# Feed-forward stages of a float32 network: the high weights multiply both parts of the rows in one 512-column product

## What is computed

```python
def rmsnorm(x, g):
    y = x * lax.rsqrt(jnp.mean(x * x, axis=-1, keepdims=True) + EPS)
    return y * g

def swiglu_2(xn, wg, wu, wd):            # wg, wu: 1024 x 2816, wd: 2816 x 1024
    return (jax.nn.silu(xn @ wg) * (xn @ wu)) @ wd

x = x + y                                # y: what the layer's mixer gives
x = x + swiglu_2(rmsnorm(x, norm_ffn[i]), ff_w_gate[i], ff_w_up[i], ff_w_down[i])
```

## Time and profile before

| | |
|---|---|
| median of 3 runs | 2932.46 us (2931.55 to 2935.47) |
| span of the profiled execution | 2930.2 us |
| around the span, against the median | 2.3 us |
| TensorE busy, matmuls | 2883.4 us (98%), 20144 |
| VectorE, ScalarE, GpSimd busy | 2031.7, 1626.6, 300.7 us |
| chain that ended last | TensorE 96% |
| moved by DMA | 613.26 MB, mean 209 GB/s |
| one 1 MB panel, issue to landing (L245) | 4.7 to 5.3 us |

### The profile page before, as it was taken

The page is one execution under the profiler, slowest core; times in us unless marked ns, Lnnn a source line. Parts: engine busy times, 40 slices in busy tenths (PEclk is TensorE's granted clock), DMA queues, the critical chain, the costliest instruction groups (busy, mean ns, idle before and its releaser), DMA issues.

```text
span 2930.2 us, 46621 instructions
## 1 busy us (share of the span) xinstructions
PE 2883.4 (98%) x20144; PEld 2666.9 (91%) x20144; DVE 2031.7 (69%) x1842; ACT 1626.6 (56%) x1603; POOL 300.7 (10%) x224
## 2 busy tenths in 40 slices
PE   8999999999999999999999999999999999999999
PEld 8999999999988888888888696999899999896999
DVE  6787665678768888888888775654665565575653
ACT  6456544545657767767767562544754454362542
POOL 1130210113010000000000002210011011002110
PEclk9999999999999999999999999999999999999999
DMA  7444555544449989889989640556365646540553
GB/s 237 159 140 155 183 180 180 187 145 144 159 173 370 350 343 375 348 339 353 377 333 373 204 154 15 180 177 210 111 187 176 198 145 186 189 144 30 158 184 119
DMA packets 359731, 613.26 MB, mean 209 GB/s; under 512 B 11520, under 2 KB 323926, under 8 KB 324577
## 3 DMA queue, kind: packets, MB, share of 16 engines
q1 hardware_dynamic: 355936, 597.99, 58.5%
q10 hardware_dynamic: 3104, 12.10, 1.2%
q0 software_dynamic: 480, 0.12, 0.0%
HBM read 608.99 MB, written 1.05 MB: 208 GB/s over the span
## 4 chain that ended last, share of the span: by engine, by line
PE 96%; DVE 1%; ACT 1%; DMA 0%; issue 0%; POOL 0%; ACTq 0%; SPq 0%; DVEq 0%; POOLq 0%
PE ps L329 19%; PE ps L331 19%; PE ps L330 19%; PE ps L1272 5%; PE ps L1274 5%; PE ps L1273 5%; PE ps L1248 3%; PE ps L1250 3%; PE ps L1249 3%; PE ps L1813 2%; PE ps L689 2%; PE ps L1828 2%; PE ps L1322 1%; PE ps L1781 1%; PE ps L1769 1%; PE ps L1291 1%
## 5 line engine op out<-in xcount | busy, mean ns | idle before, releaser
L273 DVE TENSOR_TENSOR wlo<-raw,whi 128x2048 fp32r<-128x2048 f32 (+2 forms) x574 | 1317.0, 2300 | 451.8 <-ACT whi L262 432.6
L262 ACT ACTIVATE whi<-raw 128x2048 fp32r<-128x2048 f32 (+2 forms) x574 | 1084.4, 1891 | 259.9 <-PE ps L331 136.3
L329 PE MATMUL ps<-HX,whi 128*128 128x256 f32 x1808 | 521.4, 288 | 16.3 <-DVE wlo L273 11.6
L331 PE MATMUL ps<-HX,wlo 128*128 128x256 f32 x1808 | 512.5, 283 | 0.0
L330 PE MATMUL ps<-HX,whi 128*128 128x256 f32 x1808 | 512.4, 283 | 0.0
L329 PE MATMUL ps<-HXB,whi 128*128 128x256 f32 x1760 | 501.3, 285 | 2.7 <-DVE HXB L448 2.7
L330 PE MATMUL ps<-HXB,whi 128*128 128x256 f32 x1760 | 498.6, 283 | 0.0
L331 PE MATMUL ps<-HXB,wlo 128*128 128x256 f32 x1760 | 498.6, 283 | 0.0
L329 PEld LDWEIGHTS ps<-HX,whi 128*128 128x128 f32 x1808 | 347.8, 192 | 22.6 <-ACT HX L524 10.3
L330 PEld LDWEIGHTS ps<-HX,whi 128*128 128x128 f32 x1808 | 347.9, 192 | 3.4 <-issue 3.3
L331 PEld LDWEIGHTS ps<-HX,wlo 128*128 128x128 f32 x1808 | 347.7, 192 | 0.0
(11 more groups left out here) (337 smaller groups left out, 4228.8 us busy)
## 6 DMA issues: line engine op xcount, KB each, us to landing
raw<-in_c_experts SPq DMA_DIRECT2D x264, 1024.0 KB, 4.9
raw<-in_w_in SPq DMA_DIRECT2D x71, 1024.0 KB, 5.0
raw<-in_ff_w_gate SPq DMA_DIRECT2D x44, 1024.0 KB, 5.3
raw<-in_ff_w_up SPq DMA_DIRECT2D x44, 1024.0 KB, 5.3
raw<-in_ff_w_down SPq DMA_DIRECT2D x32, 1024.0 KB, 5.2
raw<-in_dense_w SPq DMA_DIRECT2D x30, 1024.0 KB, 5.3
raw<-in_hy_w_in SPq DMA_DIRECT2D x24, 1024.0 KB, 5.3
raw<-in_ff_w_down SPq DMA_DIRECT2D x16, 768.0 KB, 4.7
```

The costliest lines, as they stand in the source:

```text
L262: e.activation(m.whi[:, i % NSPLIT, 0:n], m.raw[:, i % NRAW, 0:n], ACT.Copy).then_inc(*k.up("act", "hi", i))
L273: e.tensor_tensor(m.wlo[:, i % NRAW, 0:n], m.raw[:, i % NRAW, 0:n], hi, ALU.subtract).then_inc(*k.up("dve", "lo", i))
L329: e.matmul(o, wh, xh, start=first and t == k0, stop=False)
L331: i = e.matmul(o, wl, xh, start=False, stop=final and t == k1 - 1)
```

## The change

In the five stages wh·xh and wh·xl become one matmul: the two parts of a chunk, x[:, :, t, :], stream as 512 columns past the same wh block and fill a whole bank: columns 0 to 255 get wh·xh, 256 to 511 get wh·xl. wl·xh is a 256-column matmul as before and adds into the first half. The two halves of the bank have to be added by somebody afterwards. A block a or b now needs two banks, which `Book.pair` hands out (an even one and its neighbour); y's need one as before, and use all of it.

```diff
+def pe_both_rows(e, k, o, w, c, x, k0, k1, kx, first=True, final=True, fresh=None):
+    for t in range(k0, k1):
+        wh, wl = (v[:, t, c:c + 128] for v in w)
+        if fresh:
+            e.wait_ge(*k.at(*fresh, kx + t))
+        e.matmul(o[:, :], wh, x[:, :, kx + t, :], start=first and t == k0, stop=False)
+        i = e.matmul(o[:, 0:L], wl, x[:, 0, kx + t, :], start=False, stop=final and t == k1 - 1)
+def pe_wide_gemm(e, k, m, s, name, x, j, fresh=None):
+    i = pe_panel(e, k, m)
+    w = weights(m, i, 8, 256)
+    o = pe_take_pair(e, k, m, "g", s, name, j)
+    pe_both_rows(e, k, o[0], w, 0, x, 0, 8, 0, fresh=fresh)
+    pe_both_rows(e, k, o[1], w, 128, x, 0, 8, 0).then_inc(*k.up("mm", "g", s, name, j))
 def pe_ffn(e, k, m, s, last, after=None):
-        pe_gemm(e, k, m, s, "a", m.HXB, [j], fresh=None if j else ("hx", last))
+        pe_wide_gemm(e, k, m, s, "a", m.HXB, j, fresh=None if j else ("hx", last))
...
-                mm = pe_weights_still(e, k, o[c][:, 0:L], w, 128 * c, m.HID, ...)
+                mm = pe_both_rows(e, k, o[c], w, 128 * c, m.HID, ...)
+def act_low_sums(e, k, m, s, name, j):
+    e.wait_ge(*k.at("g", s, name, j))
...
+    e.activation(low_sums(m, name, j), pair_halves(k, m, "g", s, name, j)[1], ACT.Copy)...
 def pool_ffn(e, k, m, s, last):
+        e.wait_ge(*k.at("sum", s, "a", j))
+        e.wait_ge(*k.at("rstd", last))
+        e.tensor_tensor(v, v, m.wide_rs, ALU.mult).then_inc(*k.up("pool", "a normed", s, j))
         e.wait_ge(*k.at("sil", s, j))
         e.tensor_tensor(v, v, m.wide_rs, ALU.mult).then_inc(*k.up("pool", "sil normed", s, j))
 def dve_ffn(e, k, m, panels, s, last, nxt, after=None):
-        dve_times_norm(e, k, m, s, last, "a", j, sil)
+        if j:
+            dve_hidden_low(e, k, m, s, j - 1)
+        e.wait_ge(*k.at("low", s, "a", j))
+        e.tensor_tensor(sil..., low_sums(m, "a", j), pair_halves(k, m, "g", s, "a", j)[0], ALU.add)...
         dve_panel(e, k, m, panels)
+        e.wait_ge(*k.at("low", s, "b", j))
+        e.tensor_tensor(b, b, pair_halves(k, m, "g", s, "b", j)[0], ALU.add)...
         e.wait_ge(*k.at("sil normed", s, j))
-        e.tensor_tensor(hf, sil, ps(k, m, "g", s, "b", j)[:, :], ALU.mult)...
+        e.tensor_tensor(hf..., sil..., b, ALU.mult)...
...
             e.wait_ge(*k.at("y", s, c))
-            e.tensor_tensor(m.X[:, c, :], m.X[:, c, :], ps(k, m, "y", s, c)[:, 0:L], ALU.add)...
+            e.tensor_tensor(m.X[:, c, :], m.X[:, c, :], o[:, 0:L], ALU.add).then_inc(*k.up("dve"))
+            e.wait_ge(*k.own("dve"))
+            e.tensor_tensor(m.X[:, c, :], m.X[:, c, :], o[:, L:2 * L], ALU.add)...
```

More of the change, by code:

```diff
@@ L102, in bank, with pair @@
         self.turn += 1
-        self.before[group], self.owner[b] = self.owner[b], group
+        self.before[group], self.owner[b] = [self.owner[b]], group
+        self.bank_of[group] = b
+        return b
+    def pair(self, *group):
+        while self.turn % 2 or self.turn % 8 in self.held or self.turn % 8 + 1 in self.held:
+            self.turn += 1
+        b = self.turn % 8
+        self.turn += 2
+        self.before[group] = self.owner[b:b + 2]
+        self.owner[b:b + 2] = [group, group]
         self.bank_of[group] = b
@@ L304, in pe_take, with pe_take_pair, pair_halves @@
     b = k.bank(*group)
-    if k.before[group]:
-        e.wait_ge(*k.at("free", *k.before[group]))
+    for owner in k.before[group]:
+        if owner:
+            e.wait_ge(*k.at("free", *owner))
     return m.psum[b]
+def pe_take_pair(e, k, m, *group):
+    b = k.pair(*group)
+    for owner in dict.fromkeys(k.before[group]):
+        if owner:
+            e.wait_ge(*k.at("free", *owner))
+    return m.psum[b], m.psum[b + 1]
+def pair_halves(k, m, *group):
+    b = k.bank_of.get(group, 0)
+    both = m.banks[:, 512 * b:512 * b + 1024].rearrange("p (c h n) -> p c h n", c=2, h=2)
+    return both[:, :, 0, :], both[:, :, 1, :]
 def pe_hold(e, k, m, *group):
@@ L1041, in act_ffn @@
             act_rstd(e, k, m, last, m.rs[:, :])
[L1042 to L1049 removed]
+        else:
+            act_hidden_high(e, k, m, s, j - 1)
+            if after:
+                after(j - 1)
+        act_low_sums(e, k, m, s, "a", j)
+        act_panel(e, k, m, panels)
+        e.wait_ge(*k.at("a normed", s, j))
+        e.activation(sil, sil, ACT.Silu).then_inc(*k.up("act", "sil", s, j))
+        act_low_sums(e, k, m, s, "b", j)
+    act_hidden_high(e, k, m, s, 10)
+    if after:
+        after(10)
     for j in range(4):
@@ L2599, in pool_program @@
     pool_sums(e, k, m, "hgrn0")
-    pool_ffn(e, k, m, "ffn0")
+    pool_ffn(e, k, m, "ffn0", "hgrn0")
     pool_sums(e, k, m, "ffn0")
```

69 lines of the change are left out of this document (42 added, 27 removed).

## The result

The changed kernel takes 2903.47 us (median of 4 runs, 2898.49 to 2904.63); beside it the kernel before took 2932.81 us. The ratio is 0.9896, with a 95% interval of 0.9884 to 0.9907: 1.0% faster, 29.3 us. The median lies inside the 8-of-10 range of 2895.5 to 2907, but outside the forecast's own range of 2896 to 2901, which had 77%, and short of the 2905 to 2912 of the third rival. The profiled execution took 2904.63 us, its span 2902.8, against 2930.2 before: 27.4 us less, where the sum of the prediction had 33.65.

A forecast was written before the change was run, and what follows sets the result against it. TensorE's matmul start distances were taken to bound the kernel; 34.3 - 0.2 - 0.45 = 33.65 us saved takes 2932.46 to 2898.8 us. Own range 2896 to 2901 (77%), 8 of 10 within 2895.5 to 2907.

The forecast's parts named there:

- the third rival: Wide matmul 5 ns dearer beside the narrow one, or GpSimd's slow case costs 6 us: 2905 to 2912 us; 8%.
- What bounds the kernel: TensorE, busy in 98% of the span; time is the sum of distances between matmul starts.
- 227 + 120 = 347 ns: Five feed-forward stages: a wide plus a narrow matmul replace three of 120 ns, 360 ns a triple.
- fourth rival: Most of the 13 ns belongs to something kept, such as weight changes: time between 2932.9 and 2898.8 us; 2%.
- 13 ns per triple: Saving for each of 2640 triples in the feed-forward stages, 34.3 us in all.
- The first blocks: First block of ffn3 saves 0.14 us less (input wait, lower clock); whole loss over five stages rounded to 0.2 us.
- The readers: Other engines' added work per turn costs nothing: their chain goes round in 8.0 us where TensorE takes 11.1.
- The down projection's second addition: Costs nothing at ends of ffn0 to ffn3, covered by 0.4 us; adds 0.45 us at the kernel's end.
- The readers stop TensorE: Rival: TensorE waits 1.29 us every turn for a pair's copy and sum, 71 us, giving 2970 us; 5%.
- Two runs cost nothing: Answers a rival: reading two runs costs about a matmul's start, pair 360 ns, time stays 2932.5 plus 0.5; 5%.
- The fifth: Rival: a wide matmul hides more of the weight change than the experts' do, 2885 to 2895 us; 3%.
- upper bound of 430 ns: Wide matmul priced as a plain float32 one of 512 columns, which would cost 502 us.

The follow-up runs named there:

- the layout with one run: Changed kernel with HXB and HID laid out by chunk, then part, so the wide matmul reads one run of 512 columns: 2901.0 us, ratio 0.9892.
- The turned order: Changed kernel with the order turned around in every other pair (wide, narrow, narrow, wide): 2902.72 us, ratio 0.9895.
- the kernel with two more: Changed kernel with both of GpSimd's multiplications of a turn done twice: 2971.6 us, ratio 1.0129.
- a break each turn: Changed kernel with one more plain float32 matmul of 128 columns, into its own bank, ending each of 55 turns: 2925.49 us, ratio 0.9975.

## Why the prediction was right, point by point

The mechanism and the size of most terms held. How near the median of 2903.47 came to 2898.8 is partly luck of the draw: by the change's own profile it would be some 2897 us with every pair short, and some 2911 with all of ffn1 to ffn4 long.

**What bounds the kernel.** Right. TensorE is still busy in 98% with 2.7 us of idle time in the five stages, and putting the third matmul back gives 1.0001 of the time before.

**227 + 120 = 347 ns.** The mechanism is right and the size nearly so. The pair takes 346.67 ns in the good case, and the read of two runs costs nothing (the layout with one run has the same two values). What was saved is what a matmul costs beyond its columns, as the prediction said. Whether this belongs to the start or to the weight load that goes with each matmul stays open: the change takes away 2640 of both, and the prediction's fourth rival reckoned with loads that stay. The sign that the prediction gave, starts 227 and 120 ns apart in turn, came as 230 and 117. The mis-sized term is "13 ns per triple": 13.33 in short stretches and 6.67 in long ones, in this profile 10.4 on average. The third rival, a wide matmul some 5 ns dearer beside a narrow one, had 8%, and it came true in part: 6.67 ns, but only in 1120 of the 2560 pairs and, outside ffn0, not always the same ones. The prediction took its two prices from a row of only narrow and a row of only wide matmuls, and the sum of the two did not have to be the price of the alternation. The turned order, 348.33, lies between.

**The first blocks.** They saved 0.35 us in four stages where 16 x 13 ns each, 0.8, was expected (of the 0.2 held back, 0.14 was ffn3's). In ffn3 I expected 0.1, and 1.45 us went, mostly because the slow piece of the earlier trace rows was missing. The kernel after at that place (start of ffn3, after the wait for the last chunk):

```profile
2337.50 0.50 PE L370 MATMUL ps<-HXB,whi 128*128 128x512 f32 x1 [1.45 <-DVE HXB L498]
...
2338.35 0.44 PE L370 MATMUL ps<-HXB,whi 128*128 128x512 f32 x1
...
2339.14 0.40 PE L370 MATMUL ps<-HXB,whi 128*128 128x512 f32 x1
...
2339.49 0.40 PE L370 MATMUL ps<-HXB,whi 128*128 128x512 f32 x1
```

The wait is the same 1.45 us, but the four pairs behind it take only 1.64 us together; then it is 0.35 a pair. Before, the matmuls after the wait went 213 ns apart, 256 columns at 1.2 GHz, half the full clock. I had taken the clock of one profile for a property of the place.

**The readers.** Right, and tested from both sides. The turn is TensorE's, each sum waits for a copy and each copy for a product. The prediction took 0.05 us for a handover; its rows give 0.03 (523.32 + 0.42 = 523.74 to 523.77), which makes its 8.0 us some 7.8 and changes nothing. It left it open whether GpSimd falls beside a panel once or twice: once, in its second operation. In the timeline of VectorE and GpSimd, answering to the earlier trace rows:

```profile
2388.37 1.30 POOL L1136 TENSOR_TENSOR work<-work,rs 128x512 f32<-128x512 f32 x1 [6.49 <-DVE work L1157]
...
2389.41 2.41 DVE L284 TENSOR_TENSOR wlo<-raw,whi 128x2048 fp32r<-128x2048 f32 x1 [1.12 <-ACT whi L273]
...
2390.41 2.56 POOL L1138 TENSOR_TENSOR work<-work,rs 128x512 f32<-128x512 f32 x1 [0.74 <-ACT work L1118]
```

1.30 us nearly alone, 2.56 beside the panel, and in the kernel with two more 3.27, there the first operation and right behind a panel's start. By the Trainium skill, "SBUF — State Buffer", section "SBUF: two separate sides", the two engines lock a shared port pair against each other; the trace agrees, since the lengthened operation ends about when the panel plus its own 1.3 us do (2389.41 + 2.41 + 1.3 = 2393.1 against 2392.97). The panel pays too, 2.41 against 2.29, but not for this operation: the first one still ran when the panel started (2388.37 + 1.30 = 2389.67). In the kernel with two more, where the first operation starts 0.16 us behind the panel, the panel takes 2.29.

**The down projection's second addition.** Right at both places. At the end of ffn0 in the kernel after, VectorE, ScalarE, VectorE, answering to the earlier trace rows:

```profile
517.42 0.42 DVE L1177 TENSOR_TENSOR X<-X,ps 128x256 f32<-128x256 f32 x1 [0.81 <-PE ps L371]
517.88 0.42 DVE L1179 TENSOR_TENSOR X<-X,ps 128x256 f32<-128x256 f32 x1
...
518.33 0.51 ACT L489 ACTIVATE HX<-X,par 128x256 fp32r<-128x256 f32 x1 [1.26 <-DVE X L1179]
...
518.88 0.48 DVE L498 SCALAR_TENSOR_TENSOR HX<-X,par,HX 128x256 fp32r<-128x256 f32 x1 [0.18 <-ACT HX L489]
```

The last chunk is ready at 519.36; TensorE began at 517.22 and needs it at 519.74. 0.4 us of cover is what was foretold. And at the end of the kernel, where it is in full view, answering to the earlier trace rows:

```profile
2899.55 0.42 DVE L1177 TENSOR_TENSOR X<-X,ps 128x256 f32<-128x256 f32 x1 [1.24 <-PE ps L371]
2900.01 0.42 DVE L1179 TENSOR_TENSOR X<-X,ps 128x256 f32<-128x256 f32 x1
```

0.46 us between the two additions, for 0.45.

**The rivals.** The readers stop TensorE in every stage only with two more GpSimd operations (2971.6; that the rival's sum was 2970 is chance, its 1.29 us a turn had another cause). Two runs cost nothing. That most of the 13 ns would stay is refuted by the short pairs. The Trainium skill has a fixed cost of about 2.5 ns per matmul at full clock ("TensorE: Matmul & The Clock Gate", section "Wait — 56ns, not 53.3ns?"). The trace disagrees for matmuls like these: the third matmul, with its load and with the same columns still streamed, was worth 13.3 ns. The fifth, more saved than 13.3 ns, shows in no stretch.

**A bound that was misread.** The prediction's upper bound of 430 ns for a plain float32 matmul of 512 columns is half of what it should be. The trace lists such a matmul as two rows: the x8 of the earlier trace rows are the four matmuls of `pe_filters`, (2547.41 - 2543.97)/4 = 860 ns each. Nothing else in the sum used it.

**What stays open.** What sets short or long in strict alternation. The value holds until something else passes through TensorE, goes when two neighbours are alike, and comes in a period of four with a break each turn. In ffn0 its pieces came the same in every such profile without breaks, in the later stages they did not. An alignment of the two lengths to something that runs by its own clock would fit, and so might the banks, but neither was tried. Open is also what of the 13.3 ns is the weight load's. Whether the lower clock between ffn2 and ffn3 belongs to executions or to kernels is open too; the mean clocks leave little room for it in the gain.

## What to carry to other kernels

Where TensorE is never idle, price a change of matmuls by the distance from start to start, and take the price of a mixed sequence from a mixed sequence: the sum of two pure ones was right at best and 6.67 ns per pair too low at worst. Merging two matmuls that share their weights into a wider one saves what a matmul and its weight load cost beyond the columns, here 13 ns of 120, and the work that it moves to other engines is free as long as their round trip (9.6 us) stays under TensorE's turn (11.1). Testing that with one operation more and two more shows how far away the edge is, and a stage with other work in its turns (ffn0 here) meets it first. Before a few microseconds are explained, profile the same kernel twice and compare the stretches where nothing was changed: the long pairs (7.5 us) differ between profiles of one program, and the clock moved 3 us one way and 1.9 the other.

## What the runs showed of the hardware

- Alternating float32r matmuls of 512 and 256 columns take 346.67 or 353.33 ns a pair at clock 1.00, one value for a whole undisturbed stretch. Turned around in every other pair, and two and two, it was 348.33 in every stretch, grouped by half blocks 349.2 to 349.4, and with only 256 columns 120.0 each.
- A plain float32 matmul stands in the trace as two rows; one of 512 columns took 860 ns, where a float32r one took 227 to its next start. One of 128 columns between float32r ones costs 0.22 us, more than its own start distance of 0.14, since the wide one behind it takes 0.32 to the next start instead of 0.23.
- With about 2 us of idle TensorE in the same 16 us of code, the granted clock was 1.00 in six profiles and 0.90 in five, at a price of 1.6 us; in one more it was 1.00 and the stretch took 16.33 us. The block behind it was at 0.84 or 0.85 in five profiles, not the same five, for about 1.4 us more.
- A GpSimd multiplication of 128x512 took 1.30 us, and 2.46 us in the mean when a VectorE panel with two SBUF inputs (2.3 us) was running; in the two places read it ended 1.15 us after the panel.
